# Retention, attention and MoE layer on one core: projections packed by lifetime, an early 1.5 MB weight load, and a gather that comes out turned

## The reference, cut to what matters

```
proj = rms_norm(x) @ w_in                     # 1024 x 3072: rq rk rv rg mq mk mv
ret  = groupnorm(retention(rope(rq), rope(rk), rv)) * silu(rg)
moba = softmax attention, 8 heads, one block of 256 keys
x    = x + concat(ret, moba) @ w_out
h    = rms_norm(x)
gate = softmax(top 4 of h @ w_router)         # 32 experts
for e in experts:                             # every expert, on its tokens
    u = h[tok] @ w1[e] + b1[e]                # w1[e]: 1024 x 2048, 8 MB
    y = clamped_swiglu(u) @ w2[e] + b2[e]     # w2[e]: 1024 x 1024, 4 MB
    x[tok] += gate * y
out  = rms_norm(x)
```

## Time and profile before

| what | value |
|---|---|
| median of 3 runs | 1038.68 us (1038.46 to 1039.01) |
| the profiled execution, its time | 1039.17 us |
| its span, first to last instruction | 1037.3 us |
| TensorE busy (modelled ends) | 1020.7 us, 98% |
| VectorE, ScalarE busy | 245.4 us, 126.5 us |
| read from HBM | 422.78 MB |
| granted TensorE clock, mean | 0.997 |

### The profile page before, as it was taken

One profiled execution on the slowest core, in us unless ns is written; L12 is line 12 of the kernel. 1 busy time (PEld: TensorE's weight loads), 2 busy tenths in 40 slices (PEclk: granted clock), 3 DMA queues, 4 the chain that ended last, 5 costly groups with the idle time before them and its releaser, 6 DMA issues.

```text
span 1037.3 us, 11270 instructions
## 1 busy us (share of the span) xinstructions
PE 1020.7 (98%) x4880; PEld 409.8 (40%) x4880; DVE 245.4 (24%) x610; ACT 126.5 (12%) x246; POOL 0.2 (0%) x4
## 2 busy tenths in 40 slices
PE   9999999999999999999999999999999999999996
PEld 8888433333333333333333333333333333333331
DVE  5776332111111111111111111111111111111111
ACT  2433120000000000000000000000000000000002
POOL 0000000000000000000000000000000000000000
PEclk9999999999999999999999999999999999999999
DMA  9983999999999999999999999999999999999995
GB/s 324 365 337 143 418 376 425 426 428 426 434 432 426 438 429 427 435 427 429 434 429 433 430 428 437 429 428 435 426 432 433 429 430 433 428 436 420 430 421 227
DMA packets 36104, 424.64 MB, mean 409 GB/s; under 512 B 3176, under 2 KB 16112, under 8 KB 19536
## 3 DMA queue, kind: packets, MB, share of 16 engines
q1 hardware_dynamic: 35744, 423.51, 97.0%
q10 hardware_dynamic: 304, 0.33, 0.1%
HBM read 422.78 MB, written 1.05 MB: 409 GB/s over the span
## 4 chain that ended last, share of the span: by engine, by line
PE 90%; DMA 7%; SPq 1%; DVE 0%; another core or an unknown queue 0%; issue 0%; ACT 0%; DVEq 0%
PE PS L1837 40%; PE PS L1860 19%; DMA ring<-in_w 7%; PE PS L1442 6%; PE PS L1806 5%; PE PS L1788 5%; PE PS L1685 3%; PE PS L1645 3%; PE PS L1895 2%; PE PS L1798 2%; PE PS L1411 1%; PE PS L1780 1%; SPq L543 1%; PE PS L1388 0%; PE PS L1968 0%; PE PS L1982 0%
## 5 line engine op out<-in xcount | busy, mean ns | idle before, releaser
L1837 PE MATMUL PS<-ring,work 128*64 128x512 f32 x1976 | 433.8, 596 | 6.0 <-DMA ring<-in_w 5.5
L1837 PEld LDWEIGHTS PS<-ring,work 128*64 128x64 f32 x1976 | 139.6, 137 | 277.2 <-issue 266.5
L1860 PE MATMUL PS<-ring,work 128*64 128x512 f32 x1024 | 227.9, 596 | 0.9 <-DMA ring<-in_w 0.8
L1860 PEld LDWEIGHTS PS<-ring,work 128*64 128x64 f32 x1024 | 72.0, 137 | 153.8 <-issue 148.9
L1300 DVE TENSOR_SCALAR work<-PS 128x512 f32<-128x512 f32 x32 | 22.1, 691 | 385.4 <-PE PS L1837 385.4
L841 ACT ACTIVATE work<-work 128x512 f32<-128x512 f32 x32 | 20.2, 631 | 523.5 <-DVE work L1300 523.5
L1265 DVE TENSOR_TENSOR work<-PS,n2w 128x512 f32<-128x512 f32 x30 | 20.7, 691 | 228.5 <-PE PS L1798 228.5
L1442 PE MATMUL PS<-ring 128*128 128x256 f32 x280 | 64.5, 382 | 0.0
L1806 PE MATMUL PS<-late,work 64*128 64x512 f32 x248 | 61.9, 616 | 0.0
L1788 PE MATMUL PS<-resid,work 128*64 128x512 f32 x248 | 58.5, 592 | 0.0
L1442 PEld LDWEIGHTS PS<-ring 128*128 128x128 f32 x280 | 51.7, 190 | 7.7 <-issue 1.4
(11 more groups left out here) (196 smaller groups left out, 453.2 us busy)
## 6 DMA issues: line engine op xcount, KB each, us to landing
ring<-in_w SPq DMA_DIRECT2D x72, 4096.0 KB, 34.8
ring<-in_w SPq DMA_DIRECT2D x35, 2048.0 KB, 13.5
ring<-in_w SPq DMA_DIRECT2D x22, 1024.0 KB, 8.4
ring<-in_w_in SPq DMA_DIRECT2D x11, 1024.0 KB, 12.1
ring<-in_w_out SPq DMA_DIRECT2D x4, 1024.0 KB, 11.1
ring<-in_w SPq DMA_DIRECT2D x6, 512.0 KB, 7.0
ring<-in_w_in SPq DMA_DIRECT2D x2, 512.0 KB, 5.8
work<-in_w SPq DMA_DIRECT2D x1, 768.0 KB, 8.2
```

What stands on the lines that cost most here:

```text
L1837: last = mm(bank(b0 + v)[64 * half:64 * half + 64, :], rows[:, c, :], turned_half(w[:, v * F:(v + 1) * F], half), start=(second and c == 0 ...
L1860: last = mm(out[64 * half:64 * half + 64, :], aT_n[:, c, 64 * h:64 * h + 64], ring[:, 2 * d + c // 2, cols:cols + BANK], start=(h == 0 and ...
```

## The change

Three things. First, the projections get a packed layout: `NAT_COL` places those that do not live at the same time in the same columns (A, B and C, 512 columns each for each token tile), so that `nat` and `mixT_moba` together take two slots (16 and 17) rather than three and a half. Slot 18 and the first half of slot 19 are then free in the head, and three quarters of pair 9, the second half of expert 0's second layer (`w2_half(0, 1)`), are loaded there right behind pair 3; the last quarter follows when `t_part` is done. The order of the other pairs changes with it. Second, `gather0` takes the tokens as the stationary operand and `pick` as the moving one, so that the result comes out turned; the two copies, the eight transposes and their waits go, and the bias is added at once for both halves (`first_bias`). Third, the moved piece is one DMA of 1 MB, no longer 0.75 MB and 0.25 MB with a wait on the gather between them.

```diff
+AREA_A, AREA_B, AREA_C, NAT_COLS = 0, 512, 1024, 1536
+NAT_COL = [AREA_A, AREA_A + 256, AREA_B, AREA_B + 256, AREA_A, AREA_A + 256, AREA_B, AREA_B + 256,
+           AREA_C, AREA_C + 256, AREA_B, AREA_B + 256]
-FIRST_ORDER = [0, 1, 2, 3, 4, 5, 10, 11, 6, 8, 9, 7]
+FIRST_ORDER = [0, 1, 2, 3, 4, 5, 10, 9, 11, 8, 6, 7]
+EARLY, EARLY_COLS = 9, 3 * 1024
...
-        nat_flat = ring[:, HEAD_CHUNKS:HEAD_CHUNKS + 3, :].rearrange("p s n -> p (s n)")
-        nat = nat_flat.rearrange("p (t n) -> p t n", t=T)
-        mixT_moba = ring[:, HEAD_CHUNKS + 3, 0:4 * SEQ].rearrange("p (c n) -> p c n", c=4)
+        nat_flat = ring[:, HEAD_CHUNKS:HEAD_CHUNKS + 2, :].rearrange("p s n -> p (s n)")
+        nat = nat_flat[:, 0:T * NAT_COLS].rearrange("p (t n) -> p t n", t=T)
+        mixT_moba = nat_flat[:, T * NAT_COLS:].rearrange("p (c n) -> p c n", c=4)
...
                 elif g == 8:
                     sp.wait_ge(retT_done, 2)
-                elif g == 9:
-                    sp.wait_ge(retT_done, 2)
                     sp.wait_ge(chunk_used, HEAD_CHUNKS - 2)
+                elif g == EARLY:
+                    sp.wait_ge(chunk_used, WIN_CHUNKS)
...
                     sp.dma_start(ring[:, 2 * d + 1, :], w2_half(1, 1)[:, SLOT_COLS:]).then_inc(ahead_in, 16)
+                    sp.dma_start(early_dst[:, 0:EARLY_COLS], early_src[:, 0:EARLY_COLS]).then_inc(early_part_in, 16)
+                elif g == EARLY:
+                    sp.dma_start(early_dst[:, EARLY_COLS:], early_src[:, EARLY_COLS:]).then_inc(pair_full[EARLY], 16)
...
-            sp.dma_start(moved_w[:, BANK:], moved_src[:, BANK:]).then_inc(moved_in, 16)
-            sp.wait_ge(gather0_done, 2)
-            sp.dma_start(moved_w[:, 0:BANK], moved_src[:, 0:BANK]).then_inc(moved_end_in, 16)
+            sp.dma_start(moved_w, moved_src).then_inc(moved_in, 16)
...
-            act.wait_ge(rows0_done, 1)
-            nc.scalar.activation(gx[0:64, :], bank(4)[0:64, :], ACT.Copy).then_inc(rows0a_ready, 1)
...
-            dve.wait_ge(rows0_done, 2)
-            nc.vector.tensor_copy(gx[64:P, :], bank(4)[64:P, :]).then_inc(rows0b_ready, 1)
...
+            def first_bias():
+                for v in range(2):
+                    for half in range(2):
+                        last = mm(bank(v)[64 * half:64 * half + 64, :], bsel0[v * E:(v + 1) * E, :],
+                                  turned_half(b1_sb[v * E:(v + 1) * E, :], half), start=True, stop=False)
+                return last
...
+            def gather0(t, half):
+                for c in range(4 * half, 4 * half + 4):
+                    at = (c % 4) * SLOTS
+                    last = mm(bank(TURN0_BANK[half])[:, at:at + SLOTS], x_cols(t, c), pick[:, t, :],
+                              start=(t == 0 and c % 4 == 0), stop=(t == T - 1), skip_group_check=True)
+                return last
...
             pe.wait_ge(pick0_ready, 1)
             for half in range(2):
-                gather0_rows(0, half)
+                gather0(0, half)
...
-            bias_half(0, bsel0)
+            first_bias().then_inc(bias_done, 1)
             pe.wait_ge(pick_ready, 1)
             for half in range(2):
-                gather0_rows(1, half).then_inc(rows0_done, 1)
-            bias_half(1, bsel0).then_inc(bias_done, 1)
-            pe.wait_ge(rows0a_ready, 1)
-            turn_rows0(0)
-            pe.wait_ge(rows0b_ready, 1)
-            turn_rows0(1)
+                gather0(1, half).then_inc(gather0_done, 1)
```

More of the change, by code:

```diff
@@ L266, in layer_kernel @@
         retw = ring[:, HEAD_CHUNKS + 6, 1536:2048]
-        ret = nat[:, :, RQ:RQ + 512]
+        ret = nat[:, :, NAT_RET:NAT_RET + 512]
         h2T = work[:, 0:2048].rearrange("p (t c n) -> p t c n", t=T, c=C)
@@ L296, in layer_kernel @@
         scr = sb("scr", [P, 256])
-        gsig = nat[:, :, MK:MK + 512]
+        gsig = nat[:, :, NAT_SIG:NAT_SIG + 512]
         gatesT = scr[2 * E:3 * E, 0:SEQ]
@@ L313, in layer_kernel @@
         moved_in = sem("moved_in")
-        moved_end_in = sem("moved_end_in")
+        early_part_in = sem("early_part_in")
         ahead_in = sem("ahead_in")
@@ L472, in nat_part @@
         def nat_part(t, j):
-            return nat[:, t, CHUNK_COL[j]:CHUNK_COL[j] + WIN_COLS]
+            return nat[:, t, NAT_COL[j]:NAT_COL[j] + WIN_COLS]
         def wait_pair(eng, p):
@@ L551, in load @@
                     sp.dma_start(dst, w2_half(e - 1, down_chunk(j, k))).then_inc(pair_full[d], 16)
+            early_dst = ring[:, 2 * EARLY:2 * EARLY + 2, :].rearrange("p a n -> p (a n)")
+            early_src = w2_half(0, 1)
             for g in FIRST_ORDER:
@@ L1137, in _ @@
                 dve.wait_ge(siglu_ready, t + 1)
[L1138 to L1139 removed]
+                link(nc.vector.tensor_tensor(nat[:, t, NAT_RG:NAT_RG + 512], nat[:, t, NAT_RG:NAT_RG + 512], gsig[:, t, :], ALU.mult))
+                ins = nc.vector.tensor_tensor(nat[:, t, NAT_RG:NAT_RG + 512], nat[:, t, NAT_RG:NAT_RG + 512], retw, ALU.mult)
                 ins.then_inc(gated, 1)
@@ L1150, in _ @@
                 link(ins)
-                nc.vector.tensor_tensor(ret[:, t, :], ret[:, t, :], nat[:, t, RG:RG + 512],
+                nc.vector.tensor_tensor(ret[:, t, :], ret[:, t, :], nat[:, t, NAT_RG:NAT_RG + 512],
                                         ALU.mult).then_inc(ret_ready, 1)
@@ L1710, in turn_logits @@
                 mm(bank(LOGIT_BANK[t])[:, 0:E], lT[:, t, :], row_id, start=True, stop=True).then_inc(logits_done, 1)
-            def gather0_rows(t, half):
-                return mm(bank(4)[64 * half:64 * half + 64, :], pick[:, t, :], resid[:, t, half_cols(half)],
-                          start=(t == 0), stop=(t == T - 1))
-            def turn_rows0(half):
-                rows = slice(64 * half, 64 * half + 64)
-                gx_v = gx.rearrange("p (i s) -> p s i", s=DEAL)
-                for c in range(4):
-                    last = nc.tensor.transpose(bank(TURN0_BANK[half])[:, c * SLOTS:(c + 1) * SLOTS], gx_v[rows, c, :],
-                                               ident[rows, rows])
-                last.then_inc(gather0_done, 1)
+            def gather0(t, half):
[4 more added lines that the diff above has]
+                return last
             for s, c in last_c[0:3]:
@@ L1872, in down @@
                     pe.wait_ge(ahead_in, 16)
+                if isinstance(r, int) and g == EARLY:
+                    pe.wait_ge(early_part_in, 16)
                 if isinstance(r, int) and g in CUTS:
```

15 lines of the change are left out of this document (6 added, 9 removed).

## The result

The change makes the kernel slower: 1045.24 us median of 4 runs (1044.64 to 1046.32) against 1038.85 us for the kernel before in the same comparison (4 runs), ratio 1.0063 with a 95% interval of 1.0045 to 1.008. The prediction was 1037.7 us, with a range up to 1039.4 us. The profiled execution of the changed kernel took 1045.26 us. Of all runs in this document one was slow, an execution of early_only with 1323.66 us at a mean granted clock of 0.751, and it is left out of that kernel's ratio.

What follows compares the result with a forecast made beforehand. The stream of loads was taken to set the end, restarting with expert 0: 0.7 us earlier start plus up to 0.5 us of line, taken as 1.0 us, turns 1038.68 into 1037.7 us; range 1035.6 to 1039.4 us.

Steps and rivals of the forecast that it cites:

- What bounds the kernel: Whole kernel: the stream of loads sets the end, TensorE has 6.4 us to spare; at 141 us expert 0's start limits it.
- The early load: Head, near 76 us: 3.66 us of transfer hide in idle time; nothing counts beyond expert 0's earlier start plus 0.5 us.
- the 1.0 us foreseen: Pair 7's load, issued at 131.13 us: it would land after 7.2 us instead of 8.2 us, gaining 1.0 us.
- the 0.5 us of line at 141 us: First load after expert 0's start: 0.5 us of its 4.0 us to landing was standing in line and might be gained.
- The turned gather: Expert 0's gather: 16 records a tile at 0.12 us each, so expert 0 starts at 139.2 us, 0.7 us earlier.
- the bias with 1.02 us: Between the gather's two tiles: bias for both halves at once takes 1.02 us rather than twice 1.07 us.
- the 0.20 us for the prefix matmuls: Behind the gather's tile 0: 0.20 us added between that tile's end at 136.03 us and the bias.
- Rival C: Turned gather: weight loads stand in line with matmuls, 0.17 us a record, expert 0 0.9 us later, 1039.6 us; chance 0.12.
- break-even: Turned gather: at 0.143 us a record expert 0 would start at 139.90 us, as before; slower decides from there on.
- upper bound: Turned gather: a record takes 0.26 us, the whole 0.21 us load exposed plus 0.05 us of matmul; 1042.4 us.
- C's milder price: Turned gather: 0.17 us a record, the load's pace of 0.12 us plus 0.05 us for 64 columns; 1039.6 us.
- the exposed part of C: Turned gather: loads exposed, up to 0.26 us a record and 1042.4 us, more than 0.2% of loss; chance 0.08.

Runs made afterwards that it cites:

- early_only: The changed kernel with only the packed columns and early load, keeping the gather, bias and two moved pieces of before; 1039.66 us, ratio 1.0000 to the kernel before.
- wide_pick: The changed kernel with `pick` streamed twice, so each gather record moves 128 columns in place of 64; 1042.88 us, ratio 1.0032 to the kernel before.
- plain_step: The changed kernel with 128 neighbouring columns as the gather's stationary operand instead of every fourth (another result); 1038.53 us, ratio 0.9988 to the kernel before.
- after: The kernel with the whole change, against the kernel before; 1045.24 us, ratio 1.0063.
- gather_only: The kernel before with only the turned gather, joint bias and single moved DMA, keeping its columns, slots and pair order; 1045.49 us, ratio 1.0053 to the kernel before.
- step_8: The changed kernel with every eighth column as the gather's stationary operand instead of every fourth (another result); 1046.85 us in one run.
- turn_mm: The kernel before with the router's 16 transposes issued as plain matmuls with the identity, step 4 kept; 1046.64 us in one run.

## Why the prediction was wrong

**What bounds the kernel: right.** The stream of loads sets the end, and it restarts when expert 0 has used up its first 0.5 MB. Over all kernels with the full clock and the head of before, first cut loads from +4.5 to +10.3 us lie 895.5 to 897.0 us ahead of the end. early_only is the plainest case: 3.66 us of transfer taken out of the stretch, and 0 us at the end.

**The early load: right.** 3.66 us hide at 76 us; the DMA idles ahead of pair 7; pair 7 gains 0.8 to 0.9 us of the 1.0 us foreseen (8.2 to 7.3 or 7.4 us to landing), and the restart takes that away again. Of the 0.5 us of line at 141 us the sum took 0.3 us. In early_only the first cut load does land 0.3 us sooner (3.7 us instead of 4.0 us), but the end stays at +903.5 us. One size was off without effect: the moved 1 MB was to land at 140.8 us and landed after 7.7 us, at 134.16 + 7.7 = 141.9 us.

**The turned gather: the step that failed**, by the words "I take 0.12 us, since that row has the same operand, the same stride and the same number of columns". It measured 0.233 us, or 0.25 us when a tile's 4.0 us are divided by 16, as the sum does. The row was of transposes: it had the same operand and stride, but another operation (and 128 moving columns, which wide_pick shows to be no matter). With steps of 1 or 2 the term would have held: plain_step started expert 0 at 139.12 us, against the forecast 139.2 us, and won 0.12%. A tile was reckoned with 16 x 0.12 = 1.92 us; the two took 4.01 and 3.92 us to the next instruction's start, 2.1 and 2.0 us more.

**The clock: a term that was missing.** I reckoned the bias with 1.02 us; it took 1.99 us, because the clock had fallen to half while the gather of 64 moving columns and 0.33 us loads ran. From forecast to measurement, expert 0's start: 139.2 + 2.1 + 2.0 for the records + 0.9 for the bias = 144.2 us, measured 143.82 us. Most of the rest is the gather's start, 0.14 us earlier than reckoned (133.97 us), and the 0.20 us for the prefix matmuls, which ran inside the gather's tail. From there, two pieces of expert 0, wholly or mostly at half clock, hold the stream up by 0.9 us each. Start (+3.97 us) and these 1.8 us make 5.8 us of the 6.15 us by which the end moved against the kernel before; 0.4 us is left open.

**Rival C was the right case with too low a price.** Its break-even, 0.143 us a record, held as far as it was tried: with tiles of 2.0 us (step 1, 0.125 us a record) and 2.1 us (step 2, 0.131 us) expert 0 starts earlier than before (+5.19 and +5.39 us against +6.12), with tiles of 4.0 us (0.25 us) later. Its upper bound, 0.26 us (load of 0.21 and matmul of 0.05 us in line), was above what was measured, but the price that went with it, 3.75 us (1042.4 us), lacked the half clock: wide_pick, which keeps the full clock, ends some 3 us later than the kernel before, and the change 6.2 us later. The mechanism of C was not what happened, either. The Trainium skill (TensorE: Matmul & The Clock Gate, section The mechanism) lists weight loads as overlapping with matmuls only when their row groups differ, though the same section also lets a load into the background weight buffer go ahead of running matmuls. The runs disagree with the first and fit the second. If loads and matmuls stood in line on the same rows, doubling the moving columns would have lengthened a record; in wide_pick it stayed the same, 3.98 us for 16. The loads overlap with the matmuls here and are slow by themselves.

**The range** ended at 1039.4 us, below even C's milder price of 1039.6 us, because the exposed part of C was given 8 in 100. The bounds for the unseen record reached from 0.06 to 0.26 us, 3.75 us of time at the upper end, and nothing in the profile favoured the nearest row strongly enough to cut that off: no matmul with a step of 4 in its stationary operand stood anywhere in the trace. The trace of the kernel before did hold a sign that a step has a price: its transposes of neighbouring columns (L1503, L1780) load in 0.14 us, those with a step of 4 (L1698, L1798) in 0.21 us. Their pace hid it.

**Smaller points.** At the full clock the bias for both halves is followed by the next matmul 1.01 us after its start (136.18 to 137.19 us in plain_step), so the 1.02 us were right for that clock. The moved piece as one DMA has no run of its own; in the change TensorE reads it at 160.2 us without a wait, long after it landed at 141.9 us. TensorE's idle time from 875 to 950 us went from 4.8 to 3.2 us and did not run out.

## What to carry to other kernels

When the trace has no row of the very instruction, a row of another operation on the same operand is no better than any other bound: keep the range open to the dear end, or find a matmul with that access pattern. Here a float32 matmul whose stationary columns lie 4 or 8 elements apart cost about twice per record what neighbouring ones cost (0.23 against 0.11 us, with at most 128 moving columns), so lay the data out so that the stationary operand reads neighbouring columns. A load that is moved earlier is worth only what the next gate behind it lets through; look for the event that issues the next load, and price the change by that event.

## What the runs showed of the hardware

- The load of 128 float32 stationary columns lasts 0.192 us with step 1, 0.196 with 2, 0.330 with 4, and 0.335 with 8; from one load to the next it is 0.11, 0.12, 0.23 and 0.24 us, and 16 records take 1.98, 2.08, 3.98 and 4.00 us. A transpose's load grows from 0.14 us with step 1 to 0.21 us with step 4, but its pace only from 0.11 to 0.12 us. Why it is spared was not found.
- The slow loads (step 4) last 0.330 us and follow every 0.233 us at the full and at the half TensorE clock alike, while the bias goes from 1.09 to 1.99 us.
- Slow loads with 64 moving columns brought the clock down to half for some 10 us, across the bias and into expert 0's 512-column matmuls (after, gather_only, step_8). The same loads with 128 moving columns left it at the full clock (wide_pick, turn_mm).
- A first cut load that was issued later moved the end by about as much, but 0.4 to 1.4 us are left over in after, gather_only, step_8 and turn_mm, and no run tells their cause.
